# Prompt attention: where the softmax is normalised, how the sink enters its sum, and the sign of the row maximum

## What is computed

```
def sw_attention_core(q, k, v, qpos, kpos, sinks):
    s = einsum('bnqkgd,bnskd->bnkgqs', q, k) * HEAD_DIM ** -0.5
    mask = (rel >= 0) & (rel <= WINDOW) & (kpos >= 0)
    s = where(mask, s, -inf)
    m = maximum(max(s, axis=-1), sink)
    e = exp(s - m)
    pr = e / (sum(e, axis=-1) + exp(sink - m))
    return einsum('bnkgqs,bnskd->bnqkgd', pr, v)
```

## Time and profile before

| | |
|---|---|
| median of 3 runs | 1317.13 us |
| span of the profiled execution | 1317.6 us |
| TensorE matmul busy | 1234.7 us, 94% |
| VectorE busy | 652.5 us, 50% |
| ScalarE busy | 366.8 us, 28% |
| GpSimd busy | 409.4 us, 31% |
| mean granted clock of TensorE | 0.972 |
| chain that ended last, by engine | PE 83%, DVE 13%, issue 2% |

### The profile page before, as it was taken

The page is one execution under the profiler, slowest core; times in us unless marked ns, Lnnn a source line. Parts: engine busy times, 40 slices in busy tenths (PEclk is TensorE's granted clock), DMA queues, the critical chain, the costliest instruction groups (busy, mean ns, idle before and its releaser), DMA issues.

```text
span 1317.6 us, 19692 instructions
## 1 busy us (share of the span) xinstructions
PE 1234.7 (94%) x7688; PEld 1206.2 (92%) x7688; DVE 652.5 (50%) x1129; ACT 366.8 (28%) x757; POOL 409.4 (31%) x189
## 2 busy tenths in 40 slices
PE   4899999999989888998898999999999999999997
PEld 3899889899989888888898999999999999999997
DVE  5789774212476676766665253565114233144321
ACT  4333333333445444544451010113002011031111
POOL 2434224222221022202213433452243352434420
PEclk8999999999989898988899999999999999999999
DMA  7313526521333333333314111104332324331211
GB/s 283 100 66 114 192 84 187 153 72 33 108 92 100 100 97 96 98 96 96 103 66 164 62 58 34 44 32 186 102 107 82 113 81 131 95 99 57 74 34 50
DMA packets 135949, 129.83 MB, mean 99 GB/s; under 512 B 40319, under 2 KB 123415, under 8 KB 135887
## 3 DMA queue, kind: packets, MB, share of 16 engines
q1 hardware_dynamic: 118487, 102.25, 25.5%
q10 hardware_dynamic: 17400, 26.71, 5.4%
HBM read 93.25 MB, written 37.71 MB: 99 GB/s over the span
## 4 chain that ended last, share of the span: by engine, by line
PE 83%; DVE 13%; issue 2%; ACT 1%; DMA 1%; DVEq 0%; SPq 0%; ACTq 0%
PE ps L573 70%; PE ps L767 3%; DVE prob L1093 3%; PE ps L755 2%; PE ps L745 2%; DVE sa L989 1%; DVE xn L935 1%; DVE sa L975 1%; DVE m_lo L939 1%; DVE sa L985 1%; DVE stack L969 1%; DVE hs L977 1%; DVE stack L967 1%; PE ps L628 1%; PE ps L684 1%
## 5 line engine op out<-in xcount | busy, mean ns | idle before, releaser
L573 PE MATMUL ps<-m_hi,w_hi 128*128 128x352 f32 x2016 | 670.0, 334 | 7.5 <-DVE m_lo L939 7.5
L573 PE MATMUL ps<-m_lo,w_hi 128*128 128x352 f32 x2016 | 654.5, 325 | 0.0
L573 PE MATMUL ps<-m_hi,w_lo 128*128 128x352 f32 x2016 | 438.3, 326 | 0.0
L573 PEld LDWEIGHTS ps<-m_hi,w_hi 128*128 128x128 f32 x2016 | 385.7, 191 | 12.0 <-issue 7.8
L573 PEld LDWEIGHTS ps<-m_lo,w_hi 128*128 128x128 f32 x2016 | 385.0, 191 | 1.3 <-issue 1.2
L573 PEld LDWEIGHTS ps<-m_hi,w_lo 128*128 128x128 f32 x2016 | 347.9, 190 | 0.0
L508 POOL TENSOR_TENSOR w_hi<-raw_a,w_one 128x1024 fp32r<-128x1024 f32 x42 | 81.8, 1947 | 842.9 <-PE ps L573 607.8
L510 POOL TENSOR_TENSOR w_lo<-raw_b,w_hi 128x1024 fp32r<-128x1024 f32 x42 | 109.9, 2617 | 3.3
L510 POOL TENSOR_TENSOR w_lo<-raw_a,w_hi 128x1024 fp32r<-128x1024 f32 x42 | 109.6, 2609 | 3.3
L508 POOL TENSOR_TENSOR w_hi<-raw_b,w_one 128x1024 fp32r<-128x1024 f32 x42 | 90.3, 2151 | 0.0
L1093 DVE TENSOR_SCALAR prob<-prob,st 128x256 f32<-128x256 f32 x128 | 83.8, 717 | 1.1
(11 more groups left out here) (185 smaller groups left out, 1186.8 us busy)
## 6 DMA issues: line engine op xcount, KB each, us to landing
raw_a<-in_w_in SPq DMA_DIRECT2D x26, 512.0 KB, 3.6
raw_b<-in_w_in SPq DMA_DIRECT2D x26, 512.0 KB, 4.3
qk_d<-qkst ACTq DMA_DIRECT2D x10, 1056.0 KB, 4.1
gate_d<-gst ACTq DMA_DIRECT2D x16, 528.0 KB, 2.7
gin<-gate_d SPq DMA_DIRECT2D x16, 528.0 KB, 3.7
qt<-qk_d SPq DMA_DIRECT2D x32, 256.0 KB, 2.8
xT_d<-sa SPq DMA_DIRECT2D x4, 1056.0 KB, 7.4
yb_d<-sa SPq DMA_DIRECT2D x1, 4224.0 KB, 12.9
```

The costliest lines, as they stand in the source:

```text
L573: last = nc.tensor.matmul(ps[:, 3 * parity + c, 0:CH], w, x[:, k, CH * c:CH * c + CH], start=(k == 0 and w is wh and x is src_hi), stop=(k ...
```

## The change

Four things change, all in the attention of the prompt.

The multiplication by the reciprocal goes from VectorE to ScalarE: `normalise` is now four Copies with a scale from a column of `st`, behind a new semaphore `recip_done`; on VectorE `reciprocals` is left.

The sink becomes column 257 of each head's probabilities: `prob` gets rows of 260 columns, `sink_column` writes the (negated) sinks into the column ahead of the next unit, the exponential runs over 257 columns, and its accumulator then holds the whole sum. The exponential of the shifted sinks and the addition go.

The masked scores are written negated, and the minimum with the negated sinks is taken in place of the maximum. That is already the bias of the exponential, whose scale is -1; the negation and the subtraction go. `sinks_n` is made once, early in the program.

The two copies per unit ahead of the fused instructions become memsets of one column. ScalarE's exponentials now wait for `att_read` and `sink_put` in place of `shift_done`.

```diff
-            prob = sb("prob", [P, 2, G, 2 * P], scope=s3)
+            prob = sb("prob", [P, 2, G, PW], scope=s3)
@@ VectorE, mask_scores
                 for s in range(2):
-                    n = att_round("S", u) + s + 1
-                    dve.wait_ge(att_done, n)
-                    v.tensor_copy(st[:, slot, 5, 2 * s:2 * s + 2], sinks[:, G * kv + 2 * s:G * kv + 2 * s + 2])
+                    dve.wait_ge(att_done, att_round("S", u) + s + 1)
+                    v.memset(st[:, slot, 1, s:s + 1], 0.0)
                     for g in (2 * s, 2 * s + 1):
                         last = v.tensor_tensor_reduce(
-                            prob[:, slot, g, :], ps[:, bank, 256 * (g % 2):256 * (g % 2) + 256],
-                            msk[:, mask, :], 1.0, sinks[:, G * kv + g:G * kv + g + 1], ALU.add, ALU.max,
+                            prob[:, slot, g, 0:2 * P], ps[:, bank, 256 * (g % 2):256 * (g % 2) + 256],
+                            msk[:, mask, :], -1.0, sinks_n[:, G * kv + g:G * kv + g + 1], ALU.add, ALU.min,
                             st[:, slot, 0, g:g + 1])
                     last.then_inc(att_read, 1)
-                dve.wait_ge(att_read, n)
-                v.tensor_scalar(st[:, slot, 1, :], st[:, slot, 0, :], -1.0, None, ALU.mult)
-                v.tensor_tensor(st[:, slot, 2, :], sinks[:, G * kv:G * kv + G], st[:, slot, 0, :], ALU.subtract)\
-                    .then_inc(shift_done, 1)
@@ VectorE
-            def normalise(u, m):
+            def reciprocals(u, m):
                 dve.wait_ge(exp_done, u + 1)
-                step.did(v.tensor_tensor(st[:, slot, 0, :], st[:, slot, 3, :], st[:, slot, 4, :], ALU.add))
-                step.settle()
-                step.did(v.reciprocal(st[:, slot, 5, :], st[:, slot, 0, :]))
-                step.settle()
-                for g in range(G):
-                    last = v.tensor_scalar(prob[:, slot, g, :], prob[:, slot, g, :], st[:, slot, 5, g:g + 1],
-                                           None, ALU.mult)
-                last.then_inc(prob_done, 1)
+                v.reciprocal(st[:, slot, 5, :], st[:, slot, 3, :]).then_inc(recip_done, 1)
@@ ScalarE
+            def sink_column(m):
+                kv = m % 4
+                a.activation(prob[:, m % 2, :, 2 * P], sinks_n[:, G * kv:G * kv + G], ACT.Copy).then_inc(sink_put, 1)
+
             def exps(u, m):
                 slot = m % 2
-                act.wait_ge(shift_done, u + 1)
+                act.wait_ge(att_read, att_round("S", u) + 2)
+                act.wait_ge(sink_put, u + 1)
                 for g in range(G):
-                    a.activation(prob[:, slot, g, :], prob[:, slot, g, :], ACT.Exp, bias=st[:, slot, 1, g:g + 1],
-                                 accum_out=st[:, slot, 3, g:g + 1])
-                a.activation(st[:, slot, 4, :], st[:, slot, 2, :], ACT.Exp).then_inc(exp_done, 1)
+                    last = a.activation(prob[:, slot, g, 0:2 * P + 1], prob[:, slot, g, 0:2 * P + 1], ACT.Exp,
+                                        bias=st[:, slot, 0, g:g + 1], scale=-1.0, accum_out=st[:, slot, 3, g:g + 1])
+                last.then_inc(exp_done, 1)
+
+            def normalise(u, m):
+                slot = m % 2
+                act.wait_ge(recip_done, u + 1)
+                for g in range(G):
+                    last = a.activation(prob[:, slot, g, 0:2 * P], prob[:, slot, g, 0:2 * P], ACT.Copy,
+                                        scale=st[:, slot, 5, g:g + 1])
+                last.then_inc(prob_done, 1)
@@ ScalarE, attention_tiles
                     exps(u, m)
+                    sink_column((m + 1) % 8)
+                    normalise(u, m)
                     if m % 2:
```

More of the change, by code:

```diff
@@ L45 @@
 XKT = 2
+PW = 2 * P + 4
 SEQ_ORDER = (0, 2, 4, 6, 1, 3, 5, 7)
@@ L190, in build @@
         warm = sb("warm", [P, 2])
+        sinks_n = sb("sinks_n", [P, NH])
         kv_out = sb("kv_out", [P, 2, 2 * NKV * HD])
@@ L225, in build @@
             vt = sb("vt", [P, 2, NKV, 2 * P], F32R, scope=s3)
-            prob = sb("prob", [P, 2, G, 2 * P], scope=s3)
+            prob = sb("prob", [P, 2, G, PW], scope=s3)
             gst = sb("gst", [P, 2, T], scope=s3)
             pt_hi = [sb("pt_hi0", [P, G * P], F32R, scope=s3)]
-            p_gap = sb("p_gap", [P, 80], scope=s3)
+            p_gap = sb("p_gap", [P, 48], scope=s3)
             qt = sb("qt", [P, 2, G, P], F32R, scope=s3)
@@ L298, in build @@
         v_loaded = [sem(f"v_loaded{i}") for i in range(NKV)]
-        shift_done, exp_done, prob_done, pt_hi_done = (
-            sem("shift_done"), sem("exp_done"), sem("prob_done"), sem("pt_hi_done"))
+        sink_put, exp_done, recip_done, prob_done, pt_hi_done = (
+            sem("sink_put"), sem("exp_done"), sem("recip_done"), sem("prob_done"), sem("pt_hi_done"))
         yb_stored, yb_loaded = sem("yb_stored"), sem("yb_loaded")
@@ L308, in build @@
         out_stored = sem("out_stored")
+        sinks_negated = sem("sinks_negated")
         ssq_init, rows_init, mix_ready, p_half = (
@@ L943, in _ @@
             step.did(v.tensor_scalar(qg, qg, HD ** -0.5, None, ALU.mult))
+            v.tensor_scalar(sinks_n[:], sinks, -1.0, None, ALU.mult).then_inc(sinks_negated, 1)
             dve.wait_ge(m_ready, KT)
@@ L1105, in attention_half @@
                     split_probs(u - 1, (m - 1) % 8)
-                normalise(u, m)
+                reciprocals(u, m)
             for m in range(8):
@@ L1110, in _ @@
             with dve.Fori(1, PBLK // 2) as i:
-                step.loop(i, 1, 16)
                 for m in range(8):
                     attention_half(i, m)
-            step.leave(PBLK // 2 - 1, 16)
             end, last_tok = PBLK * NKV, slice(SEQ - P, SEQ)
@@ L1393, in _ @@
             act.wait_ge(zero_done, 2)
+            act.wait_ge(sinks_negated, 1)
             def gate(m, h, before):
@@ L1437, in attention_tiles @@
                         warmed.did(a.activation(warm[:, 1:2], warm[:, 0:1], ACT.Exp))
+            sink_column(0)
             attention_tiles(0, first=True)
```

## The result

| | before | after |
|---|---|---|
| median of 4 runs | 1316.99 us | 1254.02 us |
| ratio, 95% interval | | 0.9521 [0.9507, 0.9534] |
| span of the profiled execution | 1317.6 us | 1252.9 us |
| TensorE busy | 1234.7 us, 94% | 1215.4 us, 97% |
| VectorE busy | 652.5 us | 540.8 us |

The changed kernel is 63 us faster, 4.8%.

What follows compares the result with a forecast made beforehand. TensorE's chain was taken as the bound, with 63.1 us hanging on waits in the attention stage: 55.7 (seven waits), 5.7 (last), 1.7 (first unit). 1317.1 - 63.1 = 1254 us, range 1251 to 1267.

Steps and rivals of the forecast that it cites:

- What bounded the kernel: Attention stage: TensorE's chain of work, with 43.1 us idling in waits; with the lowered clock, 63.1 us hang on them.
- the seven waits: Attention stage: TensorE's score products wait about 5.3 us each for VectorE's gate_output; with the clock 7.96 each, 55.7 us together.
- the three terms: Gains in the attention stage: 55.7 us from seven long waits, 5.7 from the last wait, 1.7 from the first unit.
- is any of these held by GpSimd?: VectorE's remaining instructions between two units: the rows say none is held, mask operation 0.48 us, reciprocal 0.25 us inside GpSimd operations.
- The Copies: Four scaled Copies new on ScalarE: 1.70 us together, between 1.4 and 2.1, and no cost on the path.
- The slack: Gated units: hi_probs on ScalarE comes 0.2 us late, leaving 1.0 of 1.2 us cover before the value product.
- The hand-over to VectorE and back: ScalarE waits for VectorE's reciprocal between sink column (379.74) and first Copy (about 379.8): some 0.1 us.
- The threshold: Four Copies on ScalarE would begin to cost time on the path at 2.7 us together, 0.65 us a Copy.
- The units: Attention stage: a unit without a stop lasts 8.97 us between first value products; 29 units make 260.1 us.
- The first unit: Start of the attention stage: 1.7 us of waits for masked scores taken as gone; 0.7 may stay.
- the rivals: ScalarE late, 1257 to 1267, 0.08; other VectorE instruction held, 1267 to 1280, 0.05; almost no gain, 0.03; slower, 0.04.
- the slower one: ScalarE becomes the bound through a 1.28 us table load ahead of each Copy: about 1344 us, chance 0.04.

Runs made afterwards that it cites:

- the move alone: Kernel before, only the four multiplies by the reciprocal moved to ScalarE, VectorE's old small steps kept; 1255.3 us, and 1256.7 us when repeated.
- the form alone: Kernel before, only its four multiplies on VectorE rewritten to put out an accumulator too, old small steps kept; 1287.8 us, ratio 0.9772.

## Why the prediction was right

*What bounded the kernel.* Right: 43.1 us of idling and the clock behind it, together 63.1, were all that was to be had in the stage, and 62.9 were had. That the price of the clock was read from unit lengths instead of from a rule made the sum independent of how the clock comes back. It was needed: the seven waits are all of about 5.3 us, but the units that hold them are 6.8 to 8.4 us too long, so the lower clock cost between 1.5 and 3.1 us behind the same stop, and 7.96 is only their mean. That the total came out within 0.2 us is partly luck: the three terms were off by 0.4, -0.8 and 0.1 us, and the single times of either kernel spread by 3 us.

*What held VectorE.* Right, and now shown from four sides: multiplies gone from VectorE (1255), the same multiplies in another form (1253.5), GpSimd's work gone (1265 with two waits left), and everything but the multiplies changed (1312). The step "is any of these held by GpSimd?" rested on two rows, and VectorE's lines in the changed kernel's trace confirm it.

*The Copies.* Predicted 1.70 us for four from the exponential's row, measured 1.71. The rule of the Trainium skill that a multiply belongs on VectorE ("ScalarE: Activation LUTs", "Rules for kernel authors") holds for the single instruction when nothing holds it, 0.35 against 0.50 us. In this kernel GpSimd made the plain form up to 2.5 us long, and then ScalarE is the better place. It is no case against VectorE as such: in the accumulating form the multiply did as well there (1254.5 against 1254.4 us).

*The slack.* `hi_probs` 0.35 us late for the 0.2 forecast, 0.87 us left for 1.0. Two terms were too small. The hand-over to VectorE and back leaves 0.15 us between the end of the sink column (591.84) and the first Copy (591.99), for which I had put 0.06. And the gate was taken from a unit of the first round, 4.26 us; in the later rounds it lasts 4.45 (593.71 to 598.16), and did so before the change (598.21 to 602.65 in the trace of before). Against that, `hi_probs` starts 0.09 us before the dummy ends. The threshold follows: 2.6 us for the four, not 2.7. The three extra Copies fell where the sum put them, with gated units of 9.5 us in the first round and 9.7 later, as the gate's two lengths say.

*The units.* A unit lasts 9.00 us, not 8.97: 0.8 us in 29. The kernels with the memsets, the sink column and the minimum have it, with the multiplies on either engine and also with GpSimd cut short (36.0 us from chunk to chunk); the kernel before with GpSimd cut short has 35.86, and the move alone 8.96 a unit outside the held ones. It is a small cost of the new order of instructions that I haven't explained.

*The first unit* gave 2.1 for 1.7 us. None of the rivals came true; the slower one lacked its table loads, as the order had said.

*What I had wrong* lies in the experiments: that small steps held in the move alone would cost 1 us a chunk (0.3), so that the run fell below its range; the count of chunks of the next stage; and, in the form alone, that all of what is lost would be held copies, where 13 us of it lie in two chunks with none.

## What to carry to other kernels

When an engine waits at regular distances for an instruction whose maximum is many times its median, look at what runs on GpSimd at that moment, and ask first whether another form of the instruction avoids the clash: here one argument more was worth as much, with the small steps out of the way, as moving the work to another engine. The busy share of the engine that takes the work says little; what counts is how long after its present end the next engine wants the result, unit by unit. A wait of TensorE that lets its clock fall costs more than it lasts, here half as much again on the mean, but by a part that varies from one wait to the next. And where the noise lies ahead of the stage that was changed, compare the profiles from that stage's start: medians that were uncertain by 2 us became times that agree to 0.1.

## What the runs showed of the hardware

- A held multiply lasts until the running operation of GpSimd ends, and each operation lets one through. In the trace of before the four of the earlier trace rows start at 599.14, 601.43, 603.33 and 605.75 and last 2.37, 1.98, 2.50 and 0.34 us; GpSimd's operations end at 601.36, 603.26 and 605.68. The first pair of rows:

```profile
598.95 2.41 POOL L510 TENSOR_TENSOR w_lo<-raw_a,w_hi 128x1024 fp32r<-128x1024 f32 x1
```
```profile
599.14 2.37 DVE L1093 TENSOR_SCALAR prob<-prob,st 128x256 f32<-128x256 f32 x1
```

- Very small instructions of VectorE are held like large ones: a copy of 128 x 2 took up to 1652 ns (median 169, in the trace of before), a `tensor_scalar` of 128 x 4 1632 ns (170, in the move alone), an addition of two 128 x 4 in SBUF 734 ns (164, before).
- The accumulating multiply of 128 x 256 takes 475 ns and an accumulator read of 82 ns, the plain one 350 ns; the accumulating one was never held in 128 cases. In the form alone, one that ran inside an operation of GpSimd:

```profile
457.62 2.41 POOL L510 TENSOR_TENSOR w_lo<-raw_a,w_hi 128x1024 fp32r<-128x1024 f32 x1
```
```profile
457.81 0.48 DVE L1093 TENSOR_SCALAR_CACHE_REDUCE prob<-prob,st 128x256 f32<-128x256 f32 x1
```

- In the trace of before, a stop of TensorE of 5.28 us was followed by 5.9 us at 1.2 GHz (606.91 to about 612.8), one of 4.37 us by 2.7 us (695.38 to about 698.1), with TensorE busy throughout; the stop of 1.57 us in the first units, and those of 0.8 us in the run with three more Copies, left the clock at 2.4 GHz. In the form alone two stops of 0.4 and 1.6 to 1.7 us, with some 0.65 us of transposes between them, lowered it in three chunks (0.50 from about 465.1 to 468.6 us in one) and left it at 1.00 in two (424 to 428 us in one).
